# Two transformer blocks on one core: where five RMS norms scale and transpose the residual

## The chip, the core and the metric

The kernel runs on 1 core of one Trainium2 chip. Its time is the device time of an execution in microseconds (us). The engines are TensorE (PE: matrix products; its weight loads are listed as PEld), VectorE (DVE), ScalarE (ACT), GpSimd (POOL) and SyncE (SP). They run their own instruction lists and wait for one another by semaphores. Data moves between memory and the on-chip buffer (SBUF) by DMA, issued here by SP and POOL. Matmuls write to eight banks of PSUM.

## The reference, cut to what matters

Two blocks on 256 tokens of 2048 numbers, all float32. Between matrix products stands an RMS norm: each token is scaled by one number, then each column by a gain.

```python
def rmsnorm(x, g):
    y = xf * lax.rsqrt(jnp.mean(xf * xf, axis=-1, keepdims=True) + NORM_EPS)
    return (y * g.astype(jnp.float32)).astype(x.dtype)

# first block
xn = rmsnorm(h, attn_norm);  proj = xn @ w_in          # norm 0
h = h + merged @ w_out
hn = rmsnorm(h, ffn_norm)                              # norm 1
h = h + peer(hn, w_peer_query, sub_keys, down, up)     # qry = hn @ w_query, 256 rows gathered per token block
x = rmsnorm(h, final_norm)
# second block
hn = rms_norm(h, mix_norm);  proj = hn @ w_in          # norm 2
h = h + concat(att_out, rnn_out) @ w_out
hn = rms_norm(h, ffn_norm)                             # norm 3
h = h + hierarchical_moe(hn, router_group, router_expert, gate, up, down)
gate = sigmoid(rms_norm(h, ple_norm) @ w_ple_gate)     # norm 4
h = h + gate * (p @ w_ple_up)
```

The peer layer takes, for each token and head, 16 rows of two large tables. The expert layer picks 2 of 32 experts for each token.

## The kernel before

**Data.** The residual `H` holds both tiles of 128 tokens (`T2` = 2) in SBUF. A projection needs the normed tokens transposed, with the 2048 columns in 16 blocks (`KC`) of 128 on the partitions: this is `XT`. `XS` is the scaled, untransposed copy, and scratch at other times. Weights pass through `W`, four slots of 2 MB; a slot's content is a unit of 8 blocks by 512 columns, numbered `u`. `load` (L335) waits until unit `u - 4` is used (`w_used`) and issues the next. TensorE works off units in order: `unit_natural` (L541) multiplies two token tiles by a unit, 16 matmuls of 512 columns; `chunk_turned` (L552) makes transposed output, 64 matmuls of 256 columns for two units. Two sets of two banks (0 to 3) take the products in turn; a set is given back by `set_free` when it is evicted.

**A norm.** `root_mean_square` (L918, L920) on ScalarE squares both tiles of `H` with a running sum and takes the root. `scale_norm` on VectorE makes the reciprocal `rstd` (L1151), scales `H` into `XS` (L1157) and says `xs_ready`. `turn_norm` on TensorE (L523) transposes 32 blocks of `XS`, block by block into banks 4 to 7. ScalarE (`keep_norm`, L926) evicts the even and VectorE (L1160) the odd ones into `XT`, with the gains in `GT` as a scale for each partition. Then `turn_norm` waits for all evictions. For norm 3 `XS` is written in permuted order, since the packing of tokens for the experts (L827) reads it so; the gains for it are in `GT[:, 48:64]`.

**Order of the work.** Norm 0 stands at the start: SP loads `x` and all constants (identity, masks, eps), waits for ten small gain loads of POOL (L456 to L461), and then loads the first units. Stage A and B follow: 58 units of projections with attention and retention between them, by a plan written out by hand. `square` multiplies by `w_out` (units 58 to 65); `add_square` (L1290) on VectorE adds each chunk of 512 columns to `H`. Norm 1 follows, the query projection (L552), the scores, and 256 gathers with their products (L484, L488, L1393, L741). After the final norm comes norm 2, then the second block's projections, its `square` (units 94 to 101), norm 3 and the router matmuls (L808), 64 of 36 columns. VectorE then picks experts (L1512 and after), with one Exp on ScalarE (L1112); TensorE packs the tokens (L827), POOL copies windows of them (L504, L505), and a loop goes over 16 pairs of experts (L857, L881, L841). SP's loads of expert weights (L397, L398, L402) wait for slots that the loop has used. The sum of the experts is added to `H` (L1625), `moe_done` is said, and norm 4 and the last projection (L898, L907) follow.

## Time and profile before

| | before |
|---|---|
| median of 3 runs | 3636.13 us (3635.49 to 3636.9) |
| the profiled execution | 3633.61 us |
| its span, first to last instruction | 3631.8 us |
| PE busy | 3129.9 us (86%), 8924 matmuls |
| DVE busy | 1082.3 us (30%) |
| ACT busy | 494.0 us (14%) |
| POOL busy | 551.4 us (15%) |
| mean granted TensorE clock | 0.977 |
| read from memory | 988.45 MB |

Busy time is a mean over stages with different limits: in some TensorE has no gap, in others the DMA queues are full and PE counts as busy with products that wait for rows. What bounds a stage is read from the chain of work that ended last, and from what each engine's idle time ended with.

### The profile page before, as it was taken

Reading aid. Unit: us, or ns where it says so; the run is one execution under the profiler, and the core shown is the slowest. Engines: PE = TensorE matmul, PEld = TensorE weight load, DVE = VectorE, ACT = ScalarE, POOL = GpSimd, SP = SyncE. Lnnn points to the kernel's source line nnn. Section 1 sums busy time; section 2 is a strip of 40 time slices with the busy share of each in tenths; the row PEclk is TensorE's granted clock in tenths of the full one; section 3 lists DMA queues with packets and bytes.
Section 4 is the critical chain, followed back from the end, with each engine's and each line's share of the span. In section 5 each row is a group of like instructions: output and inputs, shape, how many; then the busy total and the mean of one; then the engine's idle time right before and its main releaser. Section 6 shows DMA issues by size and latency. Waiting matters only on the chain.

```text
span 3631.8 us, 25401 instructions
## 1 busy us (share of the span) xinstructions
PE 3129.9 (86%) x8924; PEld 1457.1 (40%) x8924; DVE 1082.3 (30%) x1719; ACT 494.0 (14%) x1242; POOL 551.4 (15%) x599
## 2 busy tenths in 40 slices
PE   7999999999996777777777777769998969999989
PEld 3444544444485222222222222227447443333334
DVE  1030010000004555546555555442211032222220
ACT  1010110000011212212121221121211010101010
POOL 1000000000003334334334334310000001000000
PEclk9999999999998999999999999998999979999999
DMA  6334334443433999999999999984432428999972
GB/s 233 139 116 156 134 142 147 142 159 139 146 132 158 421 421 421 421 422 421 422 421 421 421 421 422 421 340 149 141 139 89 146 94 340 422 422 422 422 306 70
DMA packets 222259, 991.85 MB, mean 273 GB/s; under 512 B 13217, under 2 KB 15697, under 8 KB 130129
## 3 DMA queue, kind: packets, MB, share of 16 engines
q0 software_dynamic: 74384, 537.49, 35.7%
q1 hardware_dynamic: 147776, 453.11, 32.9%
q8 instruction: 55, 0.90, 0.1%
q14 instruction: 44, 0.35, 0.0%
HBM read 988.45 MB, written 2.10 MB: 273 GB/s over the span
## 4 chain that ended last, share of the span: by engine, by line
PE 56%; DMA 33%; issue 3%; DVE 3%; ACT 3%; POOL 1%; SPq 0%; DVEq 0%; POOLq 0%; ACTq 0%
PE bank L541 32%; DMA W<-in_peer_expert_down,big 25%; DMA W<-in_w_expert_up 7%; PE bank L552 6%; PE bank L857 4%; PE bank L741 4%; PE bank L907 3%; DVE W L1393 1%; PE bank L841 1%; PE bank L827 1%; PE bank L523 1%; PE bank L881 1%; ACT XS L918 1%; ACT big L1047 0%; PE bank L576 0%
## 5 line engine op out<-in xcount | busy, mean ns | idle before, releaser
L541 PE MATMUL bank<-W,XT 128*128 128x512 f32 x1856 | 802.6, 592 | 0.6 <-ACT XT L926 0.6
L1393 DVE CUSTOM_DVE_ANT_0 W<-W,big 128x2048 f32<-128x2048 f32 x256 | 586.8, 2292 | 572.3 <-DMA W<-in_peer_expert_down,big 572.3
L541 PEld LDWEIGHTS bank<-W,XT 128*128 128x128 f32 x1856 | 351.2, 190 | 430.4 <-issue 428.8
L741 PE MATMUL bank<-W,big 128*128 128x512 f32 x688 | 319.7, 608 | 135.2 <-ACT big L1047 133.9
L484 POOL DMA_INDIRECT W<-in_peer_expert_down,big x256 | 252.7, 987 | 1207.3 <-DVE big L1366 1129.6
L741 PE MATMUL bank<-XT,big 128*128 128x512 f32 x688 | 317.3, 604 | 111.2 <-ACT big L1047 111.2
L741 PE MATMUL bank<-XS,big 128*128 128x512 f32 x672 | 310.0, 604 | 109.2 <-ACT big L1047 106.6
L541 PE MATMUL bank<-W,big 128*128 128x512 f32 x896 | 387.2, 594 | 3.0 <-ACT big L935 2.0
L541 PEld LDWEIGHTS bank<-W,big 128*128 128x128 f32 x896 | 170.6, 191 | 217.5 <-issue 216.2
L741 PEld LDWEIGHTS bank<-W,big 128*128 128x128 f32 x688 | 125.5, 192 | 328.6 <-issue 311.6
L741 PEld LDWEIGHTS bank<-XT,big 128*128 128x128 f32 x688 | 124.3, 190 | 304.1 <-issue 287.4
L857 PE MATMUL bank<-W,XS 128*64 128x512 f32 x1024 | 228.0, 599 | 17.2 <-DMA W<-in_w_expert_up 11.5
L741 PEld LDWEIGHTS bank<-XS,big 128*128 128x128 f32 x672 | 121.5, 190 | 297.6 <-issue 291.2
L552 PE MATMUL bank<-XT,W 128*128 128x256 f32 x1024 | 223.9, 381 | 1.7 <-DVE XT L1160 1.1
L552 PEld LDWEIGHTS bank<-XT,W 128*128 128x128 f32 x1024 | 195.6, 191 | 28.9 <-issue 1.3
L1042 ACT ACTIVATE small<-small 128x1 f32<-128x1 f32 x256 | 51.9, 203 | 991.2 <-DVE small L1393 987.4
L504 POOL COPY XS<-XT 128x448 f32 x32 | 17.9, 560 | 959.6 <-issue 589.4
L857 PEld LDWEIGHTS bank<-W,XS 128*64 128x64 f32 x1024 | 79.0, 138 | 163.6 <-issue 163.6
L841 PE MATMUL bank<-big 128*128 128x512 f32 x272 | 130.8, 612 | 0.4 <-DVE H L1625 0.4
L488 POOL DMA_INDIRECT XT<-in_peer_expert_up,big x86 | 87.2, 1014 | 231.6 <-DVE small L1393 196.6
L488 POOL DMA_INDIRECT XS<-in_peer_expert_up,big x84 | 82.4, 981 | 226.2 <-DVE small L1393 191.8
L488 POOL DMA_INDIRECT W<-in_peer_expert_up,big x86 | 81.0, 942 | 223.0 <-DVE small L1393 202.7
(299 smaller groups left out, 1759.6 us busy)
## 6 DMA issues: line engine op xcount, KB each, us to landing
W<-in_w_in SPq DMA_DIRECT2D x66, 2048.0 KB, 7.8
W<-in_w_expert_gate SPq DMA_DIRECT2D x68, 1024.0 KB, 15.0
W<-in_w_expert_up SPq DMA_DIRECT2D x68, 1024.0 KB, 17.0
big<-in_w_expert_down SPq DMA_DIRECT2D x32, 2048.0 KB, 12.6
W<-in_w_out SPq DMA_DIRECT2D x16, 2048.0 KB, 8.1
W<-in_w_ret_branch SPq DMA_DIRECT2D x8, 2048.0 KB, 8.0
W<-in_w_peer_query SPq DMA_DIRECT2D x8, 2048.0 KB, 8.1
W<-in_w_ple_gate SPq DMA_DIRECT2D x8, 2048.0 KB, 13.0
```

The costliest lines, as they stand in the source:

```text
L484: pool.indirect_dma_start(down_row(n), None, down_t, row).then_inc(down_in[n % RING], 16)
L488: pool.indirect_dma_start(up_row(n), None, up_t, row).then_inc(up_in[n % RING], 16)
L523: last = pe.transpose(bank[4 + k % 4][:, t * P:(t + 1) * P], XS[:, t, k * P:(k + 1) * P], ident)
L541: mm = pe.matmul(ps[t][:, :], lhs(k0 + k, t), w[:, k, :], start=first and k == 0, stop=last_unit and k == kn - 1)
L552: mm = pe.matmul(o, slot(u + k // 8, CH)[:, k % 8, b * P:(b + 1) * P], XT[:, :, k * P:(k + 1) * P], start=k == 0, stop=k == KC - 1)
L741: mm = pe.matmul(bank[4 * (n // P) + c][:, :], DIAG[:, n % 4, :], up_row(n)[:, c * CH:(c + 1) * CH], start=n % P == 0, stop=n % P == P - 1)
L827: mm = pe.matmul(bank[4 + k % 4][:, :], XS[:, t, k * P:(k + 1) * P], SELP[:, t, :], start=t == 0, stop=t == 1)
L841: pe.matmul(bank[t][:, :], SELT[:, buf, t * P:(t + 1) * P], YS[:, n * CH:(n + 1) * CH], start=True, stop=True).then_inc(scat_mm, 1)
L857: mm = pe.matmul(bank[2][lo:hi, :], XTE[:, p, 8 * half + k, lo:hi], moving(half, e, k), start=half == 0 and k == 0, stop=half == 1 and k == 7)
L907: mm = pe.matmul(bank[2 * (q % 2) + t][:, :], xt(8 * j + k, t), slot(u, CH)[:, k, :], start=j == 0 and k == 0, stop=j == 1 and k == 7)
L1042: act.activation(acts[:, j:j + 1], dots[:, n % BATCH:n % BATCH + 1], ACT.Gelu)
L1393: dve.tensor_tensor_reduce(out=down_row(n), in0=down_row(n), in1=HN[:, n // P, :], scale=1.0, scalar=0.0, op0=ALU.mult, op1=ALU.add, accum ...
```

## The change

The residual is transposed as it is, without the scale of the tokens, and the scale is put on when the product is evicted. Gains stay at the eviction of the transposes.

- `turn_raw` transposes `H` for norms 0, 1, 3 and 4. Norm 0 needs `x`, the identity (now a load of its own) and the first five gain loads. The rest of the constants is loaded behind the first weight unit.
- In both `square`s (now unrolled) the transposes of the chunk before lie between the two units of a chunk; the last four blocks follow the last add. For norm 3 they alternate between two banks (4, 5), and the router's matmuls (banks 6, 7) for these blocks follow the second unit. The sum of squares is made chunk by chunk on ScalarE (`keep_square`) and added up on VectorE.
- `rstd` is the `scale` of the evictions of the first block's projections, of the sigmoids of its gates, of the peer scores `S`, of the router's logits, and of the last sigmoid. `HN` for the gathers is made from `H`, `rstd` and the gains in one operation.
- For norm 3 ScalarE makes the permuted `XS` after `rstd`. The router's weights come in natural order, and the gains for the packing in `GP`.
- Norm 2 is computed as before. Only its wait for all evictions goes.
- The wait for all evictions is replaced by one for each block ahead of its first matmul (`wait_xt`), for norms 0, 1, 2 and 4. Norm 4 keeps a full wait ahead of the transposes of `PIN`.

```diff
@@ sync: order of the first loads
-            sp.dma_start(H[:, :, :], A["x"][0].rearrange("(t p) n -> p t n", p=P)).then_inc(x_loaded, 16)
-            sp.dma_start(C[:, :], consts[:, 0:CONST_W]).then_inc(c_loaded, 16)
-            sp.wait_ge(g_loaded, 10 * 16)
-            for u in range(4):
+            sp.dma_start(C[:, 0:P], consts[:, 0:P]).then_inc(ident_loaded, 16)
+            sp.dma_start(H[:, :, :], A["x"][0].rearrange("(t p) n -> p t n", p=P)).then_inc(x_loaded, 16)
+            sp.wait_ge(norm_gains_loaded, 5 * 16)
+            load(0, rows(w_in, 0, 8, 0))
+            sp.dma_start(C[:, P:], consts[:, P:CONST_W]).then_inc(c_loaded, 16)
+            for u in range(1, 4):
                 load(u, rows(w_in, 8 * (u % 2), 8, CH * (u // 2)))
@@ gpsimd: router weights in natural order, gains of the packed tokens in GP, no wait
-            pool.dma_start(WR[:, :, 0:4], A["w_router_group_2"][0].rearrange("(p k) n -> p k n", p=P)).then_inc(rows_loaded, 16)
-            pool.wait_ge(gt_ready, 2)
-            pool.dma_start(GT[:, 48:64], A["ffn_norm_2"].rearrange("o (p k) -> p (o k)", p=P)).then_inc(rows_loaded, 16)
+            pool.dma_start(WR[:, :, 0:4], A["w_router_group_2"][0].rearrange("(k p) n -> p k n", p=P)).then_inc(rows_loaded, 16)
+            pool.dma_start(GP[:, :], A["ffn_norm_2"].rearrange("o (p k) -> p (o k)", p=P)).then_inc(rows_loaded, 16)
@@ tensor
+            def turn_raw(j, ks, banks=4):
+                for k in ks:
+                    if k >= banks:
+                        pe.wait_ge(xt_dve if k % 2 else xt_act, 8 * j + (k - banks) // 2 + 1)
+                    for t in range(T2):
+                        last = pe.transpose(bank[4 + k % banks][:, t * P:(t + 1) * P], H[:, t, k * P:(k + 1) * P], ident)
+                    last.then_inc(x_turned, 1)
+            def wait_xt(j, k):
+                pe.wait_ge(xt_dve if k % 2 else xt_act, 8 * j + k // 2 + 1)
-            def square(u0, q0, lhs):
...
+            def square(u0, q0, lhs, j, banks):
+                for c in range(4):
+                    q, u = q0 + c, u0 + 2 * c
+                    wait_set(q)
+                    ps = bank[2 * (q % 2):2 * (q % 2) + 2]
+                    unit_natural(u, ps, lhs, 0, 8, True, False)
+                    if c:
+                        pe.wait_ge(set_free, CREDITS + 2 * q)
+                        turn_raw(j, range(4 * c - 4, 4 * c), banks)
+                    unit_natural(u + 1, ps, lhs, 8, 8, False, True)
+                    if c and j == 3:
+                        route(range(4 * c - 4, 4 * c))
+                pe.wait_ge(set_free, CREDITS + 2 * (q0 + 4))
+                turn_raw(j, range(12, KC), banks)
+            def route(ks):
+                for k in ks:
+                    wait_xt(3, k)
+                    for t in range(T2):
+                        mm = pe.matmul(bank[6 + t][:, 0:36], xt(k, t), WR[:, k, :], start=k == 0, stop=k == KC - 1)
+                return mm
@@ tensor: the places of the norms
-            turn_norm(0)
+            pe.wait_ge(x_loaded, 16)
+            turn_raw(0, range(KC))
-            square(UC, QCC, lambda k, t: P1[:, t, GR + k * P:GR + (k + 1) * P])
-            turn_norm(1)
+            square(UC, QCC, lambda k, t: P1[:, t, GR + k * P:GR + (k + 1) * P], 1, 4)
-            turn_norm(3)
-            for t in range(T2):
-                for k in range(KC):
-                    mm = pe.matmul(bank[4][:, 64 * t:64 * t + 36], xt(k, t), WR[:, k, :], start=k == 0, stop=k == KC - 1)
-            mm.then_inc(routed, 1)
+            route(range(12, KC)).then_inc(routed, 1)
+            pe.wait_ge(xs_ready, 4)
-            turn_norm(4)
+            pe.wait_ge(moe_done, 1)
+            turn_raw(4, range(KC))
@@ scalar
+            def keep_square(q0, j, banks):
+                for c in range(4):
+                    keep_norm(j, 4 * c, 4 * c + 4, banks)
+                    act.wait_ge(set_free, CREDITS + 2 * (q0 + c + 1))
+                    for t in range(T2):
+                        last = act.activation(XS[:, t, c * CH:(c + 1) * CH], H[:, t, c * CH:(c + 1) * CH], ACT.Square,
+                                              accum_out=parts[:, t, c:c + 1])
+                    if c == 2:
+                        act.drain()
+                        act.activation(rms, parts[:, :, 0], ACT.Sqrt)
+                last.then_inc(parts_ready, 1)
+                act.wait_ge(sum_ready, parts_of[j])
+                act.activation(rms, ss, ACT.Sqrt, scale=1.0 / D, bias=eps).then_inc(rms_ready, 1)
-                                       ACT.Silu if c * CH >= GR else ACT.Copy).then_inc(set_free, 1)
+                                       ACT.Silu if c * CH >= GR else ACT.Copy, scale=rstd[:, t:t + 1]).then_inc(set_free, 1)
@@ scalar: behind the second w_out
-            root_mean_square(set_free, CREDITS + 2 * QCH, rms_ready)
-            keep_norm(3)
+            keep_square(QCF, 3, 2)
+            act.wait_ge(rstd_ready, 3)
+            for t in range(T2):
+                act.activation(XS[:, t, :].rearrange("p (k d) -> p k d", k=KC), H[:, t, :].rearrange("p (d k) -> p k d", k=KC),
+                               ACT.Copy, scale=rstd[:, t:t + 1]).then_inc(xs_ready, 1)
@@ vector
+            def add_square(u0, q0, j, banks):
+                for c in range(4):
+                    dve.wait_ge(w_used, u0 + 2 * c + 2)
+                    for t in range(T2):
+                        h = H[:, t, c * CH:(c + 1) * CH]
+                        TT(h, bank[2 * ((q0 + c) % 2) + t][:, :], h, ALU.add).then_inc(set_free, 1)
+                    scale_turned(j, 4 * c, 4 * c + 4, banks)
-            logits = bank[4][:, 0:128].rearrange("p (t e) -> p t e", t=2)
-            dve.tensor_copy(RL[:, :, 0:4], logits[:, :, 0:4])
-            dve.tensor_copy(RL[:, :, 8:40], logits[:, :, 4:36])
+            for t in range(T2):
+                TS(RL[:, t, 0:4], bank[6 + t][:, 0:4], rstd[:, t:t + 1], None, ALU.mult)
+                TS(RL[:, t, 8:40], bank[6 + t][:, 4:36], rstd[:, t:t + 1], None, ALU.mult)
```

## Rows read from the trace of the kernel before

**Rows 1.** The page: chain shares by engine, and GB/s in 40 slices.
```profile
PE 56%; DMA 33%; issue 3%; DVE 3%; ACT 3%; POOL 1%; SPq 0%; DVEq 0%; POOLq 0%; ACTq 0%
...
GB/s 233 139 116 156 134 142 147 142 159 139 146 132 158 421 421 421 421 422 421 422 421 421 421 421 422 421 340 149 141 139 89 146 94 340 422 422 422 422 306 70
```

**Rows 2.** The chain in order of time: start us, us, what.
```profile
28.32 96.37 PE bank L541 x224
...
1011.93 110.74 PE bank L552 x512
...
2807.82 110.14 PE bank L541 x256
...
2936.21 12.40 PE bank L808 x64
...
3504.75 27.47 PE bank L907 x64
```

**Rows 3.** Timeline of POOL and SP at the start: start us, us, engine, line.
```profile
3.50 0.50 POOL L456 DMA_DIRECT2D big<-in_ple_norm  x1
...
13.48 29.39 SPq L335 DMA_DIRECT2D W<-in_w_in  x5
```

**Rows 4.** DMA view, windows at 3, 14, 3476 us (last: landing) and 13.3 to 45.
```profile
big<-in_ple_norm POOLq DMA_DIRECT2D x1, 8.0 KB, 6.3
...
W<-in_w_in SPq DMA_DIRECT2D x1, 2048.0 KB, 17.3
...
W<-in_w_ple_gate SPq DMA_DIRECT2D x1, 2048.0 KB, 17.5
...
q1 hardware_dynamic: 4303, 8.68, 80.7%
q0 software_dynamic: 281, 0.49, 12.3%
```

**Rows 5.** Timeline after the first `w_out`: adds, scaling, transposes, first eviction.
```profile
995.20 1.29 DVE L1290 TENSOR_TENSOR H<-bank,H 128x512 f32 x2 [26.18 <-PE bank L541]
...
1002.33 2.48 DVE L1157 TENSOR_SCALAR XS<-H,small 128x2048 f32<-128x2048 f32 x2
...
1004.87 5.99 PE L523 MATMUL bank<-C,XS 128*128 128x128 f32 x32 [9.82 <-DVE XS L1157]
1005.60 0.47 ACT L926 ACTIVATE XT<-bank,GT 128x256 f32<-128x256 f32 x1 [3.54 <-PE bank L523]
```

**Rows 6.** Timeline of VectorE and ScalarE after the second `w_out`, to Exp.
```profile
2925.29 3.80 DVE L1157 TENSOR_SCALAR XS<-H,small 128x2048 f32<-128x2048 f32 x2
...
2948.63 0.17 DVE L1512 COPY small<-bank 128x8 f32<-128x8 f32 x1 [12.57 <-PE bank L808]
...
2935.70 1.28 ACT L1112 ACT_TABLE_LOAD   x1
2952.72 0.21 ACT L1112 ACTIVATE small<-small 128x8 f32<-128x8 f32 x1 [15.73 <-DVEq L1539]
```

**Rows 7.** Timeline of SP: first weights of the second expert pair.
```profile
3010.41 0.35 SPq L397 DMA_DIRECT2D W<-in_w_expert_gate  x1
```

**Rows 8.** Timeline after the experts: SP, ScalarE, TensorE.
```profile
3476.39 87.13 SPq L335 DMA_DIRECT2D W<-in_w_ple_gate  x8
...
3484.71 1.91 ACT L918 ACTIVATE XS<-H 128x2048 f32<-128x2048 f32 x1 [10.00 <-DVEq L1653]
...
3493.07 6.05 PE L523 MATMUL bank<-C,XS 128*128 128x128 f32 x32 [9.16 <-DVE XS L1157]
```

**Rows 9.** Timeline of ScalarE: an eviction with a column as its scale.
```profile
2968.89 0.69 ACT L1116 ACTIVATE XT<-bank,GT 128x512 f32<-128x512 f32 x1 [15.87 <-PE bank L827]
```

**Rows 10.** Windows: us, busy (x) PE, PEld, DVE, ACT, POOL, then PEclk, DMA, GB/s.
```profile
125.00:210.00 85.00, 81.48 (x227) 38.82 (x225) 9.21 (x24) 14.26 (x37) 0.00 (x0) 1.00 0.42 149
...
2490.00:2500.00 10.00, 10.00 (x64) 9.93 (x63) 0.00 (x0) 2.37 (x3) 0.00 (x0) 0.70 0.84 300
...
2965.00:2972.00 7.00, 6.70 (x12) 3.03 (x13) 1.58 (x8) 0.69 (x1) 0.00 (x0) 0.75 0.46 157
```

More of the change, by code:

```diff
@@ L540, in unit_natural @@
                     for k in range(kn):
+                        if fresh is not None and t == 0:
+                            wait_xt(fresh, k0 + k)
                         mm = pe.matmul(ps[t][:, :], lhs(k0 + k, t), w[:, k, :],
@@ L551, in chunk_turned @@
                     for k in range(KC):
+                        if fresh is not None and b == 0:
+                            wait_xt(fresh, k)
                         mm = pe.matmul(o, slot(u + k // 8, CH)[:, k % 8, b * P:(b + 1) * P],
@@ L554, in chunk_turned @@
                 mm.then_inc(w_used, 2)
-            def square(u0, q0, lhs):
-                with pe.Fori(0, 2) as i:
-                    for c in range(2):
-                        q, u = q0 + c, u0 + 2 * c
-                        wait_set(q, i)
-                        ps = bank[2 * (q % 2):2 * (q % 2) + 2]
-                        for j in range(2):
-                            unit_natural(u + j, ps, lhs, 8 * j, 8, j == 0, j == 1, i, 4)
+            def square(u0, q0, lhs, j, banks):
[18 more added lines that the diff above has]
+                return mm
             def turn(buf, src, n):
@@ L710, in _ @@
             pe.wait_ge(turn_kept, turns)
-            square(UC, QCC, lambda k, t: P1[:, t, GR + k * P:GR + (k + 1) * P])
-            turn_norm(1)
-            with pe.Fori(0, 2) as i:
-                for c in range(2):
-                    q, u = QCD + c, UD + 2 * c
-                    wait_set(q, i)
-                    chunk_turned(u, bank[2 * (q % 2):2 * (q % 2) + 2], i, 4)
+            square(UC, QCC, lambda k, t: P1[:, t, GR + k * P:GR + (k + 1) * P], 1, 4)
+            for c in range(4):
+                q, u = QCD + c, UD + 2 * c
+                wait_set(q)
+                chunk_turned(u, bank[2 * (q % 2):2 * (q % 2) + 2], 1 if c == 0 else None)
             pe.wait_ge(keys_loaded, 16)
@@ L1508, in _ @@
             dve.memset(RL[:, :, 4:8], LOWEST)
-            scale_norm(3)
+            add_square(UF, QCF, 3, 2)
+            add_parts()
+            dve.wait_ge(rms_ready, 4)
+            dve.reciprocal(rstd, rms).then_inc(rstd_ready, 1)
+            dve.drain()
             dve.wait_ge(routed, 1)
-            logits = bank[4][:, 0:128].rearrange("p (t e) -> p t e", t=2)
-            dve.tensor_copy(RL[:, :, 0:4], logits[:, :, 0:4])
-            dve.tensor_copy(RL[:, :, 8:40], logits[:, :, 4:36])
+            for t in range(T2):
+                TS(RL[:, t, 0:4], bank[6 + t][:, 0:4], rstd[:, t:t + 1], None, ALU.mult)
+                TS(RL[:, t, 8:40], bank[6 + t][:, 4:36], rstd[:, t:t + 1], None, ALU.mult)
             dve.drain()
```

146 lines of the change are left out of this document (79 added, 67 removed).

## Prediction

> **What bounds the kernel now.** I read four views. The page's chain of work that ended last is 56% TensorE and 33% DMA, and of the 40 slices those where GB/s stands at 421 or 422 are the table gathers (slices 14 to 26) and the expert weights (35 to 38) [rows 1]. So there are two kinds of stretch. In the projections TensorE runs back to back: the chain in order of time shows stretches of 96 to 111 us without a break [rows 2]. In the gathers and experts the DMA queues are full, and TensorE's speed is worth nothing; but the moment at which such a stretch starts is worth its whole shift, since the chain runs through it. What the change touches are the five seams in which a norm stands between two stretches. There the timeline (each engine's instructions in order) shows TensorE idle while ScalarE squares, VectorE scales, and the transposes wait for both. The seams are: the start up to 28.32; after the first output projection, up to 1011.93; before the second block's projections; after the second output projection, up to the router's end; and after the experts, up to 3504.75 [rows 2]. I go through them one by one.
>
> **Seam 1, the start.** Before, SP issues the first weights at 13.48, after the gains of all ten small loads, and TensorE's first matmul starts at 28.32, behind squares, root, scaling and transposes [rows 2, 3]. Afterwards the transposes need only x, the identity and five gain loads. The last of these is issued at 3.50 and takes 6.3 us, so it lands at 9.8 [rows 3, 4]; SP can issue the first weight unit at about 9.9, and transposes (16 blocks at the eviction pace, some 7 us) end at about 17.5, ahead of it. A unit is 2.1 MB. The hardware queue moved 8.68 MB in 80.7% of 31.7 us, which makes 6.2 us for a unit; at the 422 GB/s of the full stretches it is 5.0 [rows 1, 4]. I take 5.4, nearer to the second, since the first has the small loads in it. But the constants (1.6 MB, 4.2 us) are now queued between unit 0 and unit 1, and the small router loads, which the page shows as the software queue with 12.3% of 31.7 us = 3.9 us of all engines after 13.3, now fall on the weights [rows 4]. Unit 0 lands at 18 to 22. Unit 1: bytes start at about 12.0 (my estimate, 2 us behind the issue), 5.81 MB at 5.4 us for 2.1 MB are 15.0 us, the small loads add 3 to 5, its receipt about 0.7: it lands at 30 to 33, and I take 31.7. TensorE has then done unit 0 (6.9 us) and stands waiting for it. Before, unit 1 was used from 28.32 + 6.87 = 35.2 (issued second in the row that begins at 13.48, at about 14.0, it landed 17.3 later at 31.3, early) [rows 2 to 4]. Unit 2 comes 5.4 us behind unit 1 and TensorE needs 6.9 us for one, so nothing is late after that. Gain 3.5 us, bounds 0 and 6. The scale of the tokens is ready later than before (constants by 26, two squares 3.8, table 1.3, root 0.3: about 32), but the first eviction wants it only when unit 1 is done at about 38.6: hidden, with 6 us of cover.
>
> **Seam 2, after w_out.** Before: the two adds start at 995.20 (1.29 us), then squares, root, reciprocal, scaling; transposes from 1004.87; first matmul of the query projection 1011.93 [rows 2, 5]. Afterwards, behind the last matmul: the two adds, then 8 transposes of blocks 12 to 15. A transpose costs 5.99/32 = 0.19 us [rows 5], so 1.5 us. The projection's first matmuls read blocks 0 onwards, which lie in XT; block 15 is evicted 0.73 + 0.47 us after its transpose starts (1004.87 to 1005.60, and the eviction [rows 5]), before the 15th matmul wants it. Start: 996.55 + 1.5 = 998.1, which is 13.8 us earlier. The other 24 transposes move into the projection, 3 groups of 1.55 us: 4.7 us on TensorE's path. Their evictions, the adds and the partial squares lie beside matmul units of 6.9 us on engines that stand idle there. Net 9.2 us, bounds 8 and 9.7. The wait of TensorE for the adds before each group holds up nothing: these are of the chunk before, over 6 us old. The per-block waits ahead of matmuls are met long before; I cost them at nothing, their cover is the 0.22 us of a matmul, and without it 16 waits would be some tenths of a us. The gain goes one to one to the gathers, whose start hangs on this chain.
>
> **Seam 3, before the second block.** The chain there is kept; only the wait for the last evictions goes. In seam 2 it is 1011.93 - (1004.87 + 5.99) = 1.07 us [rows 2, 5]; taken 0.8, bounds 0 and 1.1.
>
> **Seam 4, second w_out and router.** Before: matmuls end at 2807.82 + 110.14 = 2917.96; scaling 2925.29; router matmuls 2936.21 for 12.40 us; VectorE's routing starts at 2948.63 [rows 2, 6]. Afterwards adds until 2919.4 (1.29 us, as in seam 2 [rows 5]). The transposes now have two banks: blocks 12 and 13 at once, 14 only when 12 is evicted (0.73 + 0.47 + semaphore = 1.24 us after), so a group takes 2.0 us instead of 1.5. Router matmuls are 12.40/64 = 0.194 us each, 8 a group: 1.55 us. The last group: transposes 2919.4 to 2921.5, router until 2923.4. On ScalarE meanwhile: block 14 out at 2921.9, two squares of 512 columns. One of 2048 takes 1.91 us [rows 8]; less 1536 columns at its own rate leaves about 0.63, so 2923.2; VectorE's sum of the parts, the root (no table load: made at the third chunk) and the reciprocal bring 2924.1. Four small scalings in place of two copies, 0.3 us more. VectorE then stands where it stood before at 2949.0: at 2924.75, 24.2 us earlier. Off that go three groups of transposes and router matmuls inside the projection: 3 x (2.05 + 1.6) = 11.0. Moreover ScalarE now makes the permuted, scaled XS (two of 128x2048), ahead of Exp. Contiguous that is 2 x 1.9 = 3.8 us. VectorE needed 3.80 with this stride, 2.48 without (the ratio is 1.53 [rows 5, 6]), so 3.8 to 5.8; the Exp table then takes 1.28, once hidden in a pause at 2935.70 [rows 6]. ScalarE is free for Exp at 2929.5 to 2931.5; routing wants it at 2952.72 - 24 = 2928.9 [rows 6]. 1.6 us lost, bounds 0.6 and 4 (twice the contiguous time). Net 24.2 - 11.0 - 1.6 = 11.6; bounds 8 and 13. The packing matmuls want XS 12 us later: hidden.
>
> The Trainium skill (SBUF — State Buffer, section on the DMA port swizzle) says that an engine reads SBUF in lines of 16 bytes and pays for each access to a new one. The permuted read steps 64 bytes, and VectorE's 1.53 agrees [rows 5, 6]; what ScalarE pays no row shows.
>
> From there the shift must survive the experts. Their stream of weights waits for the first use of a slot (3010.41 [rows 7]), which hangs on routing, packing and the window copies, all moved alike, so the full queue starts and ends earlier by the same.
>
> **Seam 5, after the experts.** Squares start at 3484.71, transposes at 3493.07 [rows 8]. Afterwards the transposes start where the squares did: 8.4 us earlier. The rest of the seam keeps its length. The first gate weights are issued at 3476.39 and take 17.5 us: 3493.9 [rows 4, 8], and the matmuls now want them at 3504.75 - 8.4 = 3496.3: covered by 2.4 us. The sigmoid's scale needs squares that now lie beside 30 us of matmuls. Net 8.4, bounds 7 and 9.
>
> **Evictions with a scale** read from a column take ScalarE 0.69 us for 512 columns [rows 9]; two of them beside 13.7 us of matmuls are hidden, whatever they took without.
>
> **Sum.** 3.5 + 9.2 + 0.8 + 11.6 + 8.4 = 33.5 us. The profiled execution took 3633.6 (span 3631.8 and 1.8 around it), 2.5 under the median of 3636.1. So 3600.1 for a profile like this one and 3602.6 for the median. Ends: lower bounds add up to 23, upper to 38.8; not all go one way, so 3597.5 to 3611 for this case.
>
> **Rivals.** (a) The clock. TensorE falls to its lower level when it has stood idle: after the routing's pause the granted clock of 2965 to 2972 is 0.75, a mean of both levels; and beside the 64 narrow matmuls from 2490 on it is 0.70 [rows 10]. The change puts eight transposes, and in one place eight narrow matmuls as well, into dense work, eleven interruptions with the last groups. If each brought 3.5 us at half speed as at 2965 (0.75 over 7 us), each costs 1.75: 19 us, leaving 14 and 3621.7. Against it: from 125 to 210 the kernel has such groups of transposes, with pauses, between units, and the clock was 1.00 [rows 10]. I give it 10%.
>
> The Trainium skill (TensorE: Matmul & The Clock Gate, Part 4, PE-mode transpose) says that transposes do not count as activity for that clock. By this rule this rival is likelier than I make it; the row from 125 to 210 speaks against it at this mixture.
>
> (b) The expert stretch absorbs seam 4: if its weights were limited by something that does not move, 11.6 us go, leaving 22 and 3614.2. For it: the queue is full for four slices, over 360 us [rows 1]. Against: it stands empty before 3010.41 and waits for TensorE [rows 7]. 5%.
>
> (c) Seam 1 gives nothing or takes 2 us, because unit 1 comes behind the constants: 3606 to 3608, inside the range. 12%.
>
> (d) Slower: the output projections run at the lower clock level throughout, because the interruptions keep it from coming back. 220 us of dense matmuls would become up to 440: 3823. The point from which it decides: once over 33.5 us of full-speed work goes at half speed, the kernel is slower. Same row against it; 3%.
>
> (e) The change does not take effect, since a shared wait (constants, the adds, a bank) keeps the old order: a few us either way of 3636. 2%.
>
> **How the numbers follow.** The forecast has 68%, (c) 12, (a) 10, (b) 5, (d) 3, (e) 2. The range 3596 to 3614.5 takes in the forecast, (c) and most of (b) and leaves out (a), (d) and (e). 0.2%, about what a measurement can tell from no change, is 7.3 us; (a), (b), (c) and the forecast are all beyond it: faster 0.95, same 0.02, slower 0.03.
>
> **What would show it.** In the changed kernel's chain: the query projection begins about 3 us after w_out's last matmul; groups of transposes of 1.5 and 2.0 us lie in the squares with clock 1.00; routing begins some 6.5 us after w_out_2; transposes follow the experts' last add at once. Wrong would be: matmuls of 0.86 us behind a group, a wait of VectorE for Exp over 4 us, or unit 1 landing after 35.

## The result, and the profile after

| | before | changed |
|---|---|---|
| median | 3635.81 us (3634.66 to 3636.9, 4 runs) | 3597.8 us (3596.65 to 3602.64, 4 runs) |
| the profiled execution | 3633.61 us | 3602.64 us |
| its span | 3631.8 us | 3600.7 us |
| mean granted TensorE clock | 0.977 | 0.979 |

The ratio is 0.990 (0.9888 to 0.9912), which is 32 to 41 us faster; by the medians it is 38.0. The forecast was 33.5 us and 3602.6. The profiled execution of the changed kernel was the longest of its four, so the two traces differ by 31.1 us only. A second profile of the same kernel (`again`, below) has a span of 3594.5 and shows where the 6 us between the two lie.

The counts in all views are records. A float32 matmul stands there as two records and a transpose as one: the 8924 "matmuls" of the table of before are records, and the router's x64 are 32 matmuls (16 blocks, two tiles).

The chain in order of time, changed kernel (start us, us, what). These lines answer to [rows 2]; the longer stretches are cut where groups of transposes now lie in them.

```profile
17.91 4.91 issue
22.82 98.91 PE bank L558 x224
...
880.61 43.47 PE bank L558 x96
924.96 27.47 PE bank L558 x64
...
997.85 110.51 PE bank L571 x512
1112.26 9.05 PE bank L766 x64
...
2451.99 27.63 PE bank L571 x128
...
2798.80 41.47 PE bank L558 x96
...
2922.38 7.36 ACT XS L1164 x2
...
2980.04 15.84 PE bank L887 x64
...
3473.44 27.47 PE bank L942 x64
```

How to read them: take one landmark after another in both chains, and write down the lead of the changed kernel. A seam is worth what the lead grows by across it.

| landmark | before | changed | lead | by this seam, and as predicted |
|---|---|---|---|---|
| first projection starts | 28.32 | 22.82 | 5.50 | |
| its first stretch ends, next begins | 125.57 | 122.61 | 2.96 | start: 3.0 (3.5) |
| first `w_out` starts | 883.50 | 880.61 | 2.89 | |
| query projection starts | 1011.93 | 997.85 | 14.08 | after `w_out`: 11.2 (9.2) |
| first gather | 1146.45 | 1133.87 | 12.58 | scores: -1.5 (0) |
| gathers are added to `H` | 2436.23 | 2425.14 | 11.09 | gathers: -1.5 (0) |
| first matmul behind norm 2 | 2462.74 | 2451.99 | 10.75 | norm 2: -0.3 (0.8) |
| second `w_out` starts | 2807.82 | 2798.80 | 9.02 | narrow matmuls, projections: -1.7 (0) |
| first experts | 3000.29 | 2980.04 | 20.25 | `w_out_2` and router: 11.2 (11.6) |
| last experts | 3478.09 | 3456.91 | 21.18 | |
| last projection | 3504.75 | 3473.44 | 31.31 | after experts: 10.1 (8.4) |
| end of the span | 3631.8 | 3600.7 | 31.1 | |

One execution against one other mixes the change with the moment at which TensorE's clock rises behind a pause. With the profile of `again` (span 3594.5) in place of the changed kernel's first, the same ledger reads: start 4.8, first `w_out` 11.7, scores -1.5, gathers -2.3, norm 2 0.2, projections 2.2, second `w_out` and router 11.4, experts 1.0, behind them 10.1, less 0.3 at the end: 37.3 us. The three large seams stay within 0.5 us; the start, norm 2, the narrow matmuls with the projections and the gathers do not.

The seam after `w_out`: timeline of the changed kernel in the middle of the first `w_out` (start us, us, engine, line, operation, out<-in, count [idle before <- what ended it]).

```profile
923.92 1.04 PE L536 MATMUL bank<-C,H 128*128 128x128 f32 x8
...
924.34 0.91 ACT L961 ACTIVATE XT<-bank,GT 128x256 f32<-128x256 f32 x2 [43.78 <-PE bank L536]
...
924.79 7.46 PE L558 MATMUL bank<-W,big 128*128 128x512 f32 x17
```

Eight transposes stand between two units without a pause: the next matmul starts 0.87 us after the first transpose, 0.11 us for each of eight, where [rows 5] showed 0.19. The evictions lie beside matmuls. In the second `w_out`, where a group has two banks, the next unit starts 1.5 us after the last one ends (2840.27 to 2841.77), at the same full clock: there the evictions set the pace.

The router and the place where Exp now waits, same columns:

```profile
2916.76 1.87 PE L596 MATMUL bank<-WR,XT 128*128 128x36 f32 x16
...
2919.95 1.87 PE L596 MATMUL bank<-WR,XT 128*128 128x36 f32 x16
...
2922.38 7.36 ACT L1164 ACTIVATE XS<-H,small 128x2048 f32<-128x2048 f32 x2 [0.23 <-DVE small L1578]
2922.44 0.22 DVE L1582 TENSOR_SCALAR small<-bank,small 128x4 f32<-128x4 f32 x1
...
2929.75 1.28 ACT L1167 ACT_TABLE_LOAD   x1
2931.05 0.21 ACT L1167 ACTIVATE small<-small 128x8 f32<-128x8 f32 x1
...
2931.39 0.17 DVE L1612 TENSOR_REDUCE small<-small 128x2 f32<-128x8 f32 x1 [4.19 <-ACT small L1168]
```

Routing (L1582) begins 5.5 us after the last wide matmul has ended (2916.92). Then VectorE stands 4.19 us for Exp, because ScalarE is busy with `XS` until 2929.74 and loads its table behind it.

Windows of the changed kernel (us, busy and count of PE, PEld, DVE, ACT, POOL, then the granted clock, DMA share, GB/s):

```profile
22.00:24.00 2.00, 1.18 (x2) 0.69 (x3) 0.00 (x0) 0.00 (x0) 0.00 (x0) 0.50 0.97 412
...
26.00:28.00 2.00, 2.00 (x3) 0.67 (x2) 0.00 (x0) 1.45 (x1) 0.00 (x0) 0.52 1.05 387
28.00:30.00 2.00, 2.00 (x6) 0.95 (x5) 0.00 (x0) 2.00 (x3) 0.00 (x0) 1.00 1.05 385
...
915.00:932.00 17.00, 17.00 (x47) 7.96 (x46) 0.92 (x2) 2.14 (x6) 0.00 (x0) 1.00 0.52 186
...
1113.85:1115.85 2.00, 2.00 (x11) 2.00 (x11) 1.54 (x10) 1.04 (x2) 0.00 (x0) 0.50 0.00 0
...
2838.00:2860.00 22.00, 21.59 (x69) 10.92 (x68) 2.26 (x4) 2.17 (x6) 0.00 (x0) 1.00 0.40 140
```

The clock is at its full 2.4 GHz (1.00) through both kinds of group, eight transposes at 924 and transposes plus router at 2840 and 2855. It is at 1.2 GHz (0.50) for the first 5 us of the projection, where TensorE has just stood idle, and under a part of the 64 records of the score matmuls. Those begin at the full clock (1.00 from 1112.3 to 1113.0), fall to 0.50 while they run, and take 9.05 us in all, where before the same 64, after a pause of the same length, took 7.42 with this window:

```profile
1126.60:1134.00 7.40, 7.39 (x64) 7.20 (x64) 5.23 (x33) 4.18 (x7) 0.00 (x0) 1.00 0.01 2
```

### The profile page after: what moved, and what is told of

Same layout as the page of the kernel before. It is cut to its first block, busy times and chain, and to the rows that moved or that the text cites. A ratio compares the mean times of both kernels' runs of the same rounds, so it can differ in the third digit from the quotient of the medians.

```text
span 3600.7 us, 25365 instructions
## 1 busy us (share of the span) xinstructions
PE 3127.6 (87%) x8924; PEld 1451.5 (40%) x8924; DVE 1072.2 (30%) x1714; ACT 510.5 (14%) x1270; POOL 553.8 (15%) x599
## 4 chain that ended last, share of the span: by engine, by line
PE 56%; DMA 33%; issue 4%; DVE 3%; ACT 2%; POOL 2%; SPq 0%; DVEq 0%; POOLq 0%; ACTq 0%
PE bank L558 33%; DMA W<-in_peer_expert_down,big 25%; DMA W<-in_w_expert_up 7%; PE bank L571 6%; PE bank L887 4%; PE bank L776 4%; PE bank L942 3%; DVE W L1455 1%; PE bank L871 1%; PE bank L857 1%; PE bank L911 1%; DMA W<-in_peer_expert_up,big 1%; PE bank L536 0%; POOL XT L492 0%; PE bank L609 0%
## 5 line engine op out<-in xcount | busy, mean ns | idle before, releaser
L887 PE MATMUL bank<-W,XS 128*64 128x512 f32 x1024 | 227.0, 597 | 17.3 <-DMA W<-in_w_expert_up 11.6
```

What stands on the lines that cost most here:

```text
L887: mm = pe.matmul(bank[2][lo:hi, :], XTE[:, p, 8 * half + k, lo:hi], moving(half, e, k), start=half == 0 and k == 0, stop=half == 1 and k == 7)
```

## The experiments

Theory A was the ledger of the prediction, corrected by the trace after: every seam gives what its removed chain measured; the start is limited by unit 1; Exp pays for `XS`; groups in dense work don't lower the clock. Theories B and C stood against single steps of it and are in the expectations. The runs were made in three groups, and the kernel before was run beside each: 3634.26 us beside `again`, `old_loads`, `const_after_unit1` and `xs_after_exp`, 3635.29 beside `norm4_undone`, `norm1_in_a_block`, `router_twice` and `both`, 3636.0 beside the rest. The same kernel thus moved by 1.0 and 1.7 us from group to group, and a difference of that size between runs of different groups decides nothing.

**The changed kernel once more** (no edit).

> The changed kernel itself, as the base of the other three. Both theories: 3597 to 3600, that is 36 to 39 us under the kernel before. Its profiled executions tell what one of them differs from another by: the first profile was 5 us longer than the other runs. Theory A: the surplus lies in the stretch of the gathers and in the phase at which TensorE's clock comes back after the three pauses (before norm 2, before the packing, before the experts), so those stretches will differ from the first profile by 1 to 2 us each and the dense projections by under 0.3. Theory B: it lies in the interleaved projections, which then differ by several us.

Measured: 3597.94 us (3596.49 to 3599.48), ratio 0.990 (0.9886 to 0.9919). The dense stretches in the middle of projections are equal to those of the first profile. Others are not: the start gave 4.9 instead of 3.0, of which 1.0 is that the projection began at 21.86 and not at 22.82, and 0.9 its stretch (97.96 for 98.91); the narrow matmuls of the second block took 8.68 instead of 11.07, the chunk behind them 29.42 instead of 30.32. That is 5.2 of the 6.2 us between the spans. Half a microsecond each lies in the first `w_out` (43.00 for 43.47) and in the transposes of norm 2 (6.15 for 6.62), and the gathers took 0.8 more (1292.07 for 1291.27). Most of it is thus the moment at which the clock rises, as A had it; B is refuted.

**The old order of the first loads.**

```diff
-            sp.dma_start(C[:, 0:P], consts[:, 0:P]).then_inc(ident_loaded, 16)
             sp.dma_start(H[:, :, :], A["x"][0]...)
+            sp.dma_start(C[:, :], consts[:, 0:CONST_W]).then_inc(c_loaded, 16)
             sp.wait_ge(norm_gains_loaded, 5 * 16)
-            load(0, rows(w_in, 0, 8, 0))
-            sp.dma_start(C[:, P:], consts[:, P:CONST_W]).then_inc(c_loaded, 16)
-            for u in range(1, 4):
+            sp.wait_ge(g_loaded, 5 * 16)
+            for u in range(4):
...
-            pe.wait_ge(ident_loaded, 16)
+            pe.wait_ge(c_loaded, 16)
```

> The start's loads go back to the old order (x, all constants, wait for all ten gain loads, then the weights); the norm stays unscaled. Theory A: the seam is bound by the landing of weight unit 1, whatever stands before it: unit 0 lands at 25.8, unit 1 at 31.3 as in the kernel before, the transposes are done by 21, so unit 0 starts at 25.8 and unit 1 at 32.7, against 32.0 in the changed kernel: 0.7 us slower than the changed kernel, and most of the 2.9 us of this seam comes from the norm's chain alone. Theory B: the order of the loads carries the gain of the seam, and it is 3 us slower.

Measured: 3602.1 us (3600.81 to 3603.22), 4.2 more than `again`; the projection starts at 25.20, not at 21.86. So the order of the loads carries 3.3 us of the seam, as B had it; A's 0.7 came from a wait for unit 1 that isn't there. The other 3.1 us of the earlier start (28.32 to 25.20) come from the norm's chain; behind both the stretch takes 97.96 us and not 96.37, which gives 1.6 of them back.

**The constants behind unit 1.**

```diff
             load(0, rows(w_in, 0, 8, 0))
+            load(1, rows(w_in, 8, 8, 0))
             sp.dma_start(C[:, P:], consts[:, P:CONST_W]).then_inc(c_loaded, 16)
-            for u in range(1, 4):
+            for u in range(2, 4):
```

> The rest of the constants is loaded behind weight unit 1 instead of behind unit 0. Theory A: unit 1 lands some 4 us earlier, at 28, TensorE's pause of 2.4 us between units 0 and 1 goes: 2.4 us faster than the changed kernel; the squares and the root then end at about 38 and unit 1's eviction waits 2 us for them, which costs nothing since two more bank pairs are free. Theory B: the late scale stops the evictions and TensorE with them: 0 to 2 us slower.

Measured: 3598.71 us (3597.22 to 3603.4), no gain. Chain:

```profile
22.78 99.32 PE bank L559 x224
```

Unit 1 is now first in the queue behind unit 0, and the stretch is as long as before the edit (98.91). What made it longer than the 96.37 of [rows 2] is the half clock of its first 5 us, in the windows above. This refutes A's reason for the start.

**Exp ahead of `XS` on ScalarE.**

```diff
             keep_square(QCF, 3, 2)
+            act.wait_ge(route_in, 1)
+            act.activation(GEXP, GEXP, ACT.Exp)
+            act.activation(RSC[:, :, 0:1], RSC[:, :, 0:1], ACT.Exp).then_inc(route_exp, 1)
             act.wait_ge(rstd_ready, 3)
             (XS as it was)
-            act.wait_ge(route_in, 1) and the two Exp
```

> ScalarE makes the permuted XS behind the router's Exp instead of ahead of it. In the changed kernel VectorE waits 4.19 us for Exp, before 0.40. Theory A: those 3.8 us come back one to one, since the experts' start hangs on them: 3.8 us faster than the changed kernel, and XS (7.4 us) is ready 3 us before the packing wants it. Theory B: packing is then held up by XS instead, or the experts' weight stream starts no earlier: under 1 us.

Measured: 3594.36 us (3593.58 to 3597.62), 3.6 less than `again` where A said 3.8. From the start of the second `w_out` to the first experts it is 175.89 us (2794.21 to 2970.10) against 181.24 in the changed kernel (2798.80 to 2980.04). Of these 5.35 us, 3.8 are VectorE's wait for Exp (0.40 for 4.19) and 1.5 the packing matmuls, which took 29.24 us for 30.78. The packing matmuls don't miss `XS`.

**Norm 4 as before**: squares, root, `XS` scaled, then its transposes.

```diff
-            pe.wait_ge(moe_done, 1)
-            turn_raw(4, range(KC))
+            pe.wait_ge(xs_ready, 6)
+            (the same transposes, of XS)
...
-                                   bank[...], ACT.Sigmoid, scale=rstd[:, t:t + 1])
+                                   bank[...], ACT.Sigmoid)
...
+                TS(XS[:, t, :], H[:, t, :], rstd[:, t:t + 1], None, ALU.mult).then_inc(xs_ready, 1)
```

> Norm 4 as in the kernel before (squares, root, scaled XS, then transposes, full waits, no scale at the sigmoid); all else changed. Theory A: the seam is worth its chain, 8.4 us, and 1.7 us more, since transposes that follow dense work at once run at the full clock (eviction pace, no slow first matmuls): 10 us slower than the changed kernel. Theory B: only the chain counts: 8.4 us slower. Theory C: the first gate weights land too late for either: under 6 us.

Measured: 3608.97 us (3607.44 to 3612.67), 11.0 more than `again`, where A said 10. In its chain the last experts start 1.4 us later than in `again` (3452.03 for 3450.64), which is not the seam's, and 16.9 us lie between the end of the experts' last matmuls and the first of the gate:

```profile
3452.03 5.82 PE bank L871 x12
3464.48 2.49 DVE XS L1734 x2
3467.02 4.87 PE bank L923 x26
3474.72 3.70 PE bank L936 x8
```

In the changed kernel it is 7.0 us (3462.7 to 3469.7). Its timeline there, and the window around it:

```profile
3463.55 4.14 PE L536 MATMUL bank<-C,H 128*128 128x128 f32 x32 [0.83 <-DVEq L1723]
```

```profile
3456.00:3466.00 10.00, 8.77 (x34) 3.93 (x32) 7.10 (x12) 1.84 (x4) 0.00 (x0) 1.00 1.00 414
```

The seam is 9.9 us by these chains. 32 transposes take 4.14 us at a clock of 1.00, not the 6.05 of [rows 8], which began at 0.50 behind a pause of 9.16 us. That is why the seam gave 10.1, not 8.4: removing the pause in front of the transposes also made them faster.

**Norm 1 in one block behind `w_out`**, unscaled still: all 32 transposes behind the last add.

```diff
-                    if c:
+                    if c and j == 3:
                         pe.wait_ge(set_free, CREDITS + 2 * q)
                         turn_raw(j, range(4 * c - 4, 4 * c), banks)
...
-                turn_raw(j, range(12, KC), banks)
+                turn_raw(j, range(12 if j == 3 else 0, KC), banks)
...
```

> Norm 1 still unscaled, but its 16 blocks are all transposed behind the projection, not in four groups. In the changed kernel an inner group costs 0.88 us of TensorE and the last one 0.9. Theory A: three inner groups go (2.6 us less), and 16 blocks at the eviction's pace of 0.43 us take 6.9 us instead of 0.9 (6.0 more): 3.4 us slower than the changed kernel. Theory B (the clock: these transposes do not hold it): the query projection starts with 3 to 4 us at half speed as well, 5 us slower. Theory C: interleaving costs what it saves, within 1 us.

Measured: 3598.84 us (3598.26 to 3599.39), 0.9 more than `again`. Timeline:

```profile
993.71 4.14 PE L536 MATMUL bank<-C,H 128*128 128x128 f32 x32 [1.38 <-DVE H L1345]
```

From the first `w_out` matmul to the query projection it is 117.75 us (880.10 to 997.85), in `again` 116.77, in the changed kernel's first profile 117.24, and 128.43 before. C is right: putting the transposes between the units is worth 0.5 to 1 us by the traces, and beside the kernel before of its own group this run is no slower than `again` (36.5 us under it, `again` 36.3), so it may be worth nothing. Of the 11.2 us of this seam 10.7 come from transposing `H` without a wait for its scale. With four banks and the clock up a transpose costs TensorE 0.11 us between the units and 0.13 in a block of 32.

**The router's matmuls twice**, logits halved.

```diff
-                        mm = pe.matmul(bank[6 + t][:, 0:36], xt(k, t), WR[:, k, :], start=..., stop=...)
+                        for again in range(2):
+                            mm = pe.matmul(bank[6 + t][:, 0:36], xt(k, t), WR[:, k, :], start=..., stop=...)
```

> Each router matmul is issued twice (the logits are halved again, so the output is the same): 64 more records among the dense ones, in groups of 16. Theory A: the clock holds at 2.4 GHz in this mixture, a record costs 0.117 us as in the changed kernel: 7.5 us slower. Theory B: the narrow work lets the clock fall, as 64 of them in a row before did (0.194 us each): 12.4 us for them and some us of dense work at half speed besides, 14 us slower or more.

Measured: 3607.68 us (3603.32 to 3610.33), 9.7 more than `again` (8.7 by the two runs of the kernel before), between A's and B's. Windows:

```profile
2885.00:2889.00 4.00, 4.00 (x34) 3.69 (x33) 1.29 (x2) 0.00 (x0) 0.00 (x0) 0.97 0.72 233
2889.00:2892.00 3.00, 3.00 (x5) 1.35 (x4) 0.00 (x0) 0.00 (x0) 0.00 (x0) 0.50 0.93 363
...
2924.70:2931.40 6.70, 6.67 (x33) 6.53 (x31) 0.81 (x3) 6.24 (x8) 0.00 (x0) 0.50 0.30 119
```

Each inner group of 32 records takes 3.50 us where 16 took 1.87. Behind the second of the three the clock falls inside dense work (0.50 from 2889), behind the third it falls as well (0.53 from 2922.8 to 2924.7), and the last group runs at half clock: 6.69 us against 1.87. So the rival of a falling clock was not empty: with 16 narrow records behind a dense unit it doesn't happen in any window I read, with twice that it does in two of three places.

**The router's matmuls all behind the last transposes** (64 records in one row, as before the change, so that only the place differs from the changed kernel).

```diff
-                    if c and j == 3:
-                        route(range(4 * c - 4, 4 * c))
...
-            route(range(12, KC)).then_inc(routed, 1)
+            route(range(KC)).then_inc(routed, 1)
```

> The transposes of norm 3 stay interleaved, but all 16 blocks of router matmuls follow the last group, where only the last four did. Theory A: a record costs 0.11 us inside or behind, so moving 48 records changes nothing as long as the clock holds; behind, the dense work has ended and the last records run at half clock (0.19 us), so 1 to 4 us slower, and VectorE's reciprocal is no longer what its routing waits for. Theory B: the router in between saves its whole time before, 12.4 us, less the last group: over 8 us slower.

Measured: 3599.51 us (3597.31 to 3603.36), ratio 0.990 (0.9883 to 0.9913): 1.6 over `again`, which decides nothing between groups; A had said 1 to 4 slower, B over 8. Timeline:

```profile
2916.58 11.17 PE L594 MATMUL bank<-WR,XT 128*128 128x36 f32 x64
...
2919.00 7.40 ACT L1162 ACTIVATE XS<-H,small 128x2048 f32<-128x2048 f32 x2 [0.23 <-DVE small L1576]
...
2932.93 0.16 DVE L1610 TENSOR_REDUCE small<-small 128x2 f32<-128x8 f32 x1 [0.40 <-ACT small L1166]
```

From the second `w_out` to the first experts it takes 181.83 us, the changed kernel 181.24. The 64 matmuls end later, but `XS` is then hidden behind them: VectorE waits 0.40 us for Exp and not 4.19. In the changed kernel as it stands, taking the router apart and the loss at Exp cancel each other. What the router's place is worth with Exp first, no run shows.

**Exp first, and the small router loads behind unit 0.** To the edit of `xs_after_exp` comes one line on GpSimd:

```diff
             pool.dma_start(rowc[:, 144:272], A["k_norm_2"].to_broadcast([P, P])).then_inc(rows_loaded, 16)
+            pool.wait_ge(w_loaded[0], 16)
             pool.dma_start(WR[:, :, 0:4], A["w_router_group_2"][0]...).then_inc(rows_loaded, 16)
```

> Exp ahead of the permuted XS, and in addition the small router loads of POOL wait until weight unit 0 has landed. In the changed kernel unit 0 lands 13.2 us after its issue with those loads beside it, and TensorE's first 5 us run at half clock after a pause of 4.7 us. Theory A: unit 0 lands at about 18, right behind the transposes, and the clock stays up: 4 us from the landing and up to 2.5 from the clock, so 4 to 6.5 us faster than the kernel with Exp first alone. Theory B: the small loads are not what delays it (unit 0 still lands at 21 or later): under 1 us.

Measured: 3589.16 us (3584.76 to 3589.97), ratio 0.987 (0.9857 to 0.9887), 5.2 less than `xs_after_exp` (6.2 by the two runs of the kernel before), inside A's 4 to 6.5. Issue of unit 0 in the changed kernel and here (last number: us to landing), and the chain here:

```profile
W<-in_w_in SPq DMA_DIRECT2D x1, 2048.0 KB, 13.2
```

```profile
W<-in_w_in SPq DMA_DIRECT2D x1, 2048.0 KB, 8.2
```

```profile
18.16 96.37 PE bank L559 x224
```

The start is 4.7 us earlier than in the changed kernel and the stretch 2.5 us shorter: without the pause behind the transposes the granted clock is 1.00 in every window from 16 to 24 us. Four small loads, 0.36 MB together (router weights, the gains `GP`, and the columns `WF` of the second `w_in`), had held up the one load that the chain waited for. Which of the four does it was not tried.

**TensorE kept busy in its pauses.** `both`, and unread matmuls of the identity with constants into a free bank: 21 ahead of norm 2's transposes, 11 and 4 during routing, 4 before the experts.

```diff
+            def idle_work(n):
+                for _ in range(n):
+                    pe.matmul(bank[0][:, :], ident, C[:, 0:CH], start=True, stop=True)
...
+            idle_work(21)
             turn_norm(2)
...
             route(range(12, KC)).then_inc(routed, 1)
+            idle_work(11)
```

> As the kernel with Exp first and late small loads, and TensorE multiplies constants into a free bank in three of its pauses (21 matmuls ahead of norm 2's transposes, 11 and 4 during the routing, 4 ahead of the experts); nobody reads them. Theory A: what the fallen clock costs behind these pauses is 4 us at the second block's gates and first chunk (11.1 for 7.0), 2.6 in the chunk behind it (30.2 for 27.6), 1 in the transposes, 1.8 in the packing and 3 at the first experts: 8 to 12 us faster than that kernel. Theory B: the slow matmuls there have another cause (weights arriving, evictions), or the time is given back to the experts' weight stream: under 3 us.

Measured: 3579.29 us (3576.42 to 3582.26), ratio 0.985 (0.9835 to 0.9862), 9.9 less than `both` (10.6 by the two runs of the kernel before), inside A's 8 to 12; mean clock 0.990, 0.981 in `both`. Chains from norm 2 on, of `both`:

```profile
2437.17 6.52 PE bank L528 x32
2443.70 27.63 PE bank L572 x128
2471.33 11.15 PE bank L809 x64
2482.48 30.22 PE bank L572 x128
...
2931.37 29.28 PE bank L858 x64
2966.32 16.79 PE bank L888 x64
```

and of `kept_busy`:

```profile
2436.06 4.14 PE bank L528 x32
2440.20 27.64 PE bank L577 x128
2467.84 8.52 PE bank L815 x64
2476.37 29.58 PE bank L577 x128
...
2923.11 27.72 PE bank L866 x64
2956.50 13.95 PE bank L897 x64
```

Every stretch behind a filled pause is shorter, and those that were dense (27.64) are not. The transposes give 2.4 us, the narrow matmuls 2.6, the packing 1.6, the first experts 2.8. Filling the pause did not keep the clock up through the 64 narrow records at 2467.84: it is 1.00 up to 2472, 0.50 from 2474 to 2478 in the middle of work without a gap, and the chunk behind still takes 29.58 us. So a pause is not the only place where the clock falls here; it also fell inside a row of narrow matmuls. This is the best version that I ran: 56.7 us under the kernel before by the medians of its group.

The Trainium skill (TensorE: Matmul & The Clock Gate, HAM oscillation) says that a burst behind a long wait begins throttled and advises against idle gaps between bursts. These runs agree: 6.52 us for the transposes behind a pause, 4.14 behind unread matmuls.

**The kernel before once more** (no edit, one execution).

> The kernel before, for a second profile. In all profiles of the changed kernel and its variants the 64 narrow matmuls of the peer scores take 9.05 us, partly at half clock, in the one profile of before 7.42 at full clock; and the time from the first gather to the sum is 1.2 to 2.3 us longer. Theory A: both belong to the change (there the clock has not fallen at norm 1): again 7.42, and a gather stretch of 1289.8 within 0.5. Theory B: chance of one execution: 9.05 and 1291 to 1292.

Measured: 3635.52 us. The score matmuls took 7.43 us, so the 7.42 of the first profile was no accident of one execution, and from the first gather to the sum in `H` it took 1289.66 us, as in the first (1289.78). In the changed kernel it is 1291.27, and 1290.6 to 1292.1 in the ten other profiles of it and its variants. A is right: both belong to the change.

## Why the prediction was right, by its own steps

**Right in its sum.** The terms were 3.5, 9.2, 0.8, 11.6 and 8.4, 33.5 us together; the same places measured 3.0, 11.2, -0.3, 11.2 and 10.1, 35.2, less 4.7 at places that I had priced at nothing, plus 0.9 on the way through the experts, less 0.3 in two small shifts: the profile's 31.1. The median says 38.0, and the profile of `again` 37.3; most of the difference is the moment at which the clock rose in one execution. The forecast of 33.5 lies between the two profiles, 4.5 us short of the median, whose 3597.8 is near the lower end of the range. That it is this close is in part luck: seams 1 and 4 are each a sum of errors that nearly cancel.

**Seam 1: the size held, the reason fell.** I had a unit at 6.9 us of TensorE and concluded that unit 1 would be late. Its landing was right: 31.9 (10.54 issued, 21.4 to landing) for my 31.7, though nothing shows the receipt of 0.7 in it by itself. But 16 matmuls are 32 records of 0.43 us in the trace, 13.7 us: the row of [rows 2] with x224 in 96.37 us is seven units, not fourteen. Unit 1 is never waited for, and `const_after_unit1` shows it. What binds is unit 0, which landed at 22.7 (9.49 issued, 13.2 to landing) and not at 18 to 22, because of the small loads that I had put on unit 1; and the 4.91 us pause cost 2.5 us more by the half clock. The two errors nearly cancelled in this execution; in `again` the seam gave 4.9.

**Seam 2: mis-sized by 2 us, on the good side.** I priced a transpose at 0.19 us from [rows 5], a group of eight at 1.55. Inside dense work eight took 0.88, so three groups cost 2.6 and not 4.7. The row of before was itself one at lowered clock, since it stood behind a pause: at full clock 32 take 4.14. The mechanism (no wait for squares, scale and copy) was right, and `norm1_in_a_block` shows that it is nearly all of the seam.

**Seam 3: -0.3 where I had 0.8, and not to be told from nothing.** The wait for the last evictions went, but from the first transpose to the first matmul it took 6.62 us against 6.28 before; in `again` 6.15, in the second profile of before 6.69, in the other variants 5.30 to 6.56, and in `kept_busy`, with most of the pause filled, 4.14. A gain below 1 us behind a pause is smaller than that spread.

**Seam 4: right by errors that cancel.** Count from the end of the last wide matmul to the moment VectorE looks for the maximum: 31.0 us before (2917.96 to 2949.00) and 6.3 changed (2916.92 to 2923.18), 24.8 us less, where I had 24.2. The groups inside the projection cost 8.0 us (118.1 for 110.1), not 11.0: transposes 1.5 us a group (I had 2.0), and the third group of the router lies beside the last adds. A router group, too, was right by two errors: I counted 8 matmuls at 0.194 us; there are 16 records at 0.109 to 0.117, 1.87 us for my 1.55. This far the seam gives 16.8 us, and I had 13.2. But Exp cost 3.8, near the upper bound of 4, not 1.6, and the packing matmuls, which I had left as they were, took 30.78 us for 29.32. With 0.3 us of small shifts that makes the 11.2. `XS` with its stride of 64 bytes took 3.68 us a tile; the nearest contiguous row of ScalarE is a square, 1.91 [rows 8]. That is a factor of 1.93, where VectorE's was 1.53 [rows 5, 6]. I had taken a value between; the nearest row was another engine's, and it misled. `xs_after_exp` got it back.

The Trainium skill (SBUF — State Buffer, section on the DMA port swizzle) says that each access to another line of 16 bytes costs. ScalarE's factor of 1.93 agrees in direction, and is larger than VectorE's.

**Seam 5: mis-sized by 1.7 us**, for the reason of seam 2: `norm4_undone` measures the seam at 9.9 by its chain.

**What I had not priced**: the scores' matmuls, 9.05 us against 7.42, at 0.50 of the clock in the window where before it was 1.00; the same 9.05 stands in `again`, `xs_after_exp`, `router_behind`, `both` and `kept_busy`, and in all other variants, so it is no accident, though neither the pause in front (3.9 us in both kernels) nor TensorE's instructions differ; the evictions of the scores now carry a scale, and no run separates that. What moved the clock's fall there stays open. So do the gathers, 0.8 to 2.4 us longer in the profiles of the changed kernel and its variants: I found no cause in the trace and tried none.

**The rivals.** (a), eleven falls of the clock, is refuted: 1.00 at 915 to 932 and 2838 to 2860. By the rule of the Trainium skill (TensorE: Matmul & The Clock Gate, Part 4, PE-mode transpose) that transposes don't count as activity, it should have been near; with eight transposes between two units of 32 records the trace shows nothing of it. The trace of before even speaks against it: at 1004.87, behind 9.82 us without work, TensorE does nothing but transposes, and the granted clock is 0.50 up to 1008.9 and 1.00 from 1009.4, still among transposes. What `router_twice` adds is plain narrow matmuls, not transposes, and there the clock did fall. (b), the experts absorbing seam 4, is refuted by the lead: 20.25 going in, 21.18 coming out. (c) is refuted in its reason, though the start did come 0.5 us short. (d) and (e) didn't come.

**My own signs.** The query projection begins 2.5 us after `w_out`'s last matmul (about 3 forecast), groups of transposes take 0.9 and 1.5 us (1.5 and 2.0) at a clock of 1.00, routing begins 5.5 us after the second `w_out` (6.5), and unit 1 lands at 31.9. One of the signs for being wrong did come: VectorE waits 4.19 us for Exp, and I had put the limit at 4. It points at the term of seam 4 that failed.

## What to carry to other kernels

A norm between two products need not stop TensorE: transpose the raw residual as soon as it is summed, and put the token's scale on at the next eviction; this was worth 10 to 11 us in each of three seams, and placing the transposes between the units at most 1 more. Only the last of the three was taken back by itself (`norm4_undone`); for the other two the price is the difference of the chains before and after. Before you take a duration from a row behind a pause, look at the granted clock there: the same instruction inside dense work cost 0.6 to 0.7 of it (a transpose 0.11 to 0.13 us for 0.19, a narrow record 0.11 to 0.12 for 0.19). When a short function on an engine is waited for and a long one is not, issue the short one first, and ask the same of small loads beside the large one that the chain waits for (3.6 and 5.2 us here).

## What the runs showed that I had not expected

- A float32 matmul stands in the trace as two records. 16 matmuls of 512 columns are 32 records and 13.7 us. A transpose stands as one.
- Unread matmuls in TensorE's pauses made the kernel 9.9 us faster (3589.16 to 3579.29), though it has 9004 records of matmuls and not 8924; the mean granted clock rose from 0.981 to 0.990.
- The clock can fall under narrow matmuls without a pause (`kept_busy` at 2474, `router_twice` at 2889), and it rose among transposes alone (before, at 1009.4).
- ScalarE pays more than VectorE for a read with a stride of 64 bytes: 3.68 us for a scaled copy against 1.91 for a contiguous square of 128x2048, VectorE 1.90 against 1.24 for the same operation.
- Four small loads, 0.36 MB in all, beside a load of 2 MB stretched its landing from 8.2 to 13.2 us.
